# A hybrid attention and mixture-of-experts block: gate and up projections from float32r halves, rows stored modulated, down projection in two banks, last stage in place

## The chip, the cores and the metric

The kernel runs on one core of a Trainium2 chip. The metric is the device time of one execution in microseconds (us), lower is better. A version's time is the median of its runs: the kernel before took 1997.77 us, the median of three runs from 1996.19 to 1998.21.

## The reference

The input is 2048 tokens of width 1024, in float32, and a conditioning vector from which six rows of 1024 come (shift, scale and gate, for each of two halves of the layer). What is computed, cut to what the change touches (`mixed` comes from attention and a short convolution):

```python
mod = silu(c) @ w_ada + b_ada
sh1, sc1, g1, sh2, sc2, g2 = split(mod, 6)
...
x  = x + g1 * (mixed @ w_out)
h2 = rms_norm(x, norm2_g) * (1 + sc2) + sh2
g  = h2 @ w_rg + b_rg                      # 4 groups: the best one is taken
e  = h2 @ w_re + b_re                      # 8 experts in each: the best two of that group
y  = sum over the two experts of gate * ((silu(h2 @ w_gate[e]) * (h2 @ w_up[e])) @ w_down[e])
x  = x + g2 * y
out = rms_norm(x, final_g)
```

There are 32 experts. Each has `w_gate` and `w_up` of 1024x256 and `w_down` of 256x1024: 1 MB each, 96 MB in all, and all of it is read.

## The kernel before, in words

The program is a sequence of stages: projection, attention, mixing (`mix`), ranking of the tokens (`route`), experts (`experts`, L1720) and the last norm (`combine`, L2126). Within a stage the instructions of each engine are written out by hand, engine by engine, and the engines wait for each other by semaphores; an engine takes its instructions strictly in the order written. TensorE is PE, VectorE DVE, ScalarE ACT, GpSimd POOL and SyncE SP.

**Products from halves.** A plain float32 product shows as two records in the trace. In the earlier stages, and in the experts' down projection, both factors are instead split into a high part, which is the value written as float32r, and a low part, which is the rest. Three float32r products (high by high, low by high, high by low) then give the result. ScalarE writes high parts and VectorE or GpSimd subtracts to get low ones.

**`mix`** takes 16 tiles of 128 tokens. For a tile TensorE multiplies the two halves of `mixed` with `w_out` (L1347), VectorE adds both to the residual (`add_attention`, and `add_conv` at L1450 to L1465), and a row `xs`, the residual divided by its root mean square, is stored for the experts. TensorE also turns the rows for the router (`turn_x`) and computes the router's logits (`route`), one and two tiles later. Because `xs` is not yet scaled by `norm2_g * (1 + sc2)` nor shifted by `sh2`, these two are brought to columns at the first tiles: 32 products of one column (`modulation_columns`, L1411) and two sums into `modc`. VectorE then scales the router's weights (`router_scale`, L1493, `wr` to `wrs`), and TensorE multiplies the shift with the weights (`router_shift`, L1418) for a bias that VectorE adds (L1490). The rows of the gates `g1` and `g2` come by row sums over `macc`, two products each (`modulation_rows`, L1405). ScalarE's queue loads the router's weights and biases (L1522 to L1527). The splits of the tiles are at L1533 (ScalarE, high) and L1573 (GpSimd, low).

**`experts`** gives each expert 192 places (`CAP`) for its tokens and works through 16 pairs of experts. A pair's tokens are gathered by GpSimd's indirect transfers: 128 for the even expert, 128 for the odd one, and the remaining 64 of both as one block `xb`. TensorE transposes the blocks in 24 products (L1864 for the even expert with the shared block, 16; L1874 for the odd one, 8) into two banks. VectorE empties the one bank (`copy_in`, L1945) and ScalarE the other (L2080), and both apply scale and shift from `modc` on the way. `gate_up` (L1877 to L1888) then does 32 float32 products of 192 columns, 16 for gate and 16 for up (`KF` is 2 blocks of 128 of the 256 columns, `KD` 8 slices of the 1024):

```python
for w, out, done in ((wg, gate, gate_done), (wu, up, up_done)):
    for f in range(KF):
        for k in range(KD):
            pe.matmul(out[:, f * CAP:(f + 1) * CAP], w[:, b, k, f * P:(f + 1) * P],
                      xT[:, k, cols_of[b]], start=k == 0, stop=k == KD - 1)
```

ScalarE applies silu to gate (L2104), VectorE multiplies with up and splits the result into `ahi` and `alo` (`middle`, L1970 to L1980), and `down` (L1890 to L1894) does 12 products of 512 columns for the first 128 tokens of an expert into two banks (`outa`), and 12 for the other 64 into two more (`outb`). VectorE empties each pair of banks in one instruction of 1024 columns that also multiplies with the token's gate and with `g2row` (`out_first`, `out_rest`, L1983 to L1995), and GpSimd adds the rows to the residual in HBM by indirect transfers (`scatter`). The down weights are split by ScalarE (L2099, 128x2048) and VectorE (L1966). The weights have two buffers each (`wg`, `wu`, `wd`); SP loads gate and up of an expert as soon as the expert two before has done its up products, and the down weights once its split is done (L1774 to L1782).

The order on TensorE is: gate and up of the odd expert, 8 transposes for the next even one, first part of down of the even expert, 8 transposes, the rest of that down, gate and up of the next even expert, 8 transposes for the next odd one, both parts of down of the odd expert (L1923 to L1939). The orders on VectorE (L2052 to L2074) and ScalarE (L2108 to L2123) follow it.

**`combine`** loads the 8 MB of the residual with eight transfers, norms tile by tile into four result buffers `res`, and stores 16 tiles; from the fifth tile on VectorE waits until a result buffer has been stored.

## Time and profile before

| what | value |
|---|---|
| median of three runs | 1997.77 us (1996.19 to 1998.21) |
| the profiled execution: its own time, its span | 1996.46 us, 1994.3 us |
| PE busy | 1801.4 us, 90% |
| DVE busy | 1179.6 us, 59% |
| ACT busy | 855.5 us, 43% |
| POOL busy | 855.5 us, 43% |
| mean DMA traffic over the span | 138 GB/s |
| mixing stage, about | 1063 to 1330 us |
| expert stage, about | 1354 to 1940 us |
| last stage, about | 1949 to 1994 us |

How to read it: one execution was taken by the hardware profiler. Its times count from the start of its span, and its own time is a little longer than the span. "Busy" counts the time in which an engine executes; waits, register and issuing instructions are not in it. In a timeline a row gives start, duration, engine, line, operation, out<-in and shape, and "x32" says that 32 records are put together. Matrix products are given as stationary shape, then moving shape. PEld are the loads of the stationary operand. In a table of stretches the columns are the window and its length, then the busy time of TensorE's products, its weight loads, VectorE, ScalarE and GpSimd, each with the number of instructions, then the granted clock of TensorE as a part of full speed, the mean busy share of the DMA engines, and GB/s.

### The profile page before, as it was taken

To read this page: it belongs to the slowest core of one execution; us is meant where nothing else is said; L and a number is where in the kernel's file an instruction comes from. 1 tells how busy PE (TensorE), PEld (TensorE's weight loads), DVE (VectorE), ACT (ScalarE), POOL (GpSimd) and SP (SyncE) were. 2 spreads that over 40 slices of the span, in tenths; PEclk is the share of its full clock that TensorE was granted. 3 is DMA by queue.
4 is the path that set the end of the run, shared out by engine and by line. 5 is a ranking of instruction groups with operands and counts; after the bars stand their busy time and mean duration, and the time that the engine had idled before them with its cause. 6 is when DMAs were issued, how large, how long until landed. Compare 5 with 4: busy or idle time off the path is not lost. (4 is left out here: it accounts for less than half of the span.)

```text
span 1994.3 us, 26932 instructions
## 1 busy us (share of the span) xinstructions
PE 1801.4 (90%) x8988; PEld 1479.5 (74%) x8988; DVE 1179.6 (59%) x2009; ACT 855.5 (43%) x1520; POOL 855.5 (43%) x887
## 2 busy tenths in 40 slices
PE   2899999997999999999995999965999999999980
PEld 2677878774777777777784788855899898999970
DVE  4597989857666666666644656553444444444444
ACT  3535454326676777677684232311222222222114
POOL 0032314103888888888892111112343443434330
PEclk8899999996999999999997999976999999999995
DMA  7656565530000000000005343414888787878848
GB/s 282 197 143 192 168 181 158 147 102 0 6 9 6 9 8 6 9 9 6 11 9 199 126 158 137 148 43 163 248 248 252 231 248 245 248 236 239 242 94 337
DMA packets 216176, 274.28 MB, mean 138 GB/s; under 512 B 28469, under 2 KB 176144, under 8 KB 215834
## 3 DMA queue, kind: packets, MB, share of 16 engines
q1 hardware_dynamic: 193498, 220.59, 34.1%
q0 software_dynamic: 20224, 52.47, 10.4%
q8 instruction: 43, 0.70, 0.1%
q10 hardware_dynamic: 2368, 0.17, 0.1%
q14 instruction: 43, 0.35, 0.1%
HBM read 229.13 MB, written 60.82 MB: 145 GB/s over the span
## 5 line engine op out<-in xcount | busy, mean ns | idle before, releaser
L1212 POOL TENSOR_TENSOR plo<-KR,phi 128x512 fp32r<-128x512 f32 (+1 forms) x320 | 353.1, 1123 | 44.6 <-ACT KR L1171 44.4
L1020 DVE TENSOR_REDUCE cmax<-tbank 128x1 f32<-128x512 f32 (+2 forms) x320 | 193.3, 605 | 106.8 <-PE tbank L835 101.6
L1170 ACT ACTIVATE phi<-tbank 128x512 fp32r<-128x512 f32 (+1 forms) x320 | 170.9, 534 | 141.8 <-PE tbank L884 137.3
L387 PE MATMUL pbank<-hhi,wslhi 128*128 128x512 f32 x512 | 207.7, 406 | 8.5 <-DVE wsllo L440 8.5
L1946 DVE TENSOR_SCALAR xTe<-ebank,modcol 128x256 f32<-128x256 f32 (+1 forms) x128 | 53.6, 471 | 262.2 <-PE ebank L1864 137.8
L387 PE MATMUL pbank<-hhi,wsllo 128*128 128x512 f32 x512 | 201.5, 394 | 0.0
L387 PE MATMUL pbank<-hlo,wslhi 128*128 128x512 f32 x512 | 201.4, 393 | 0.0
L331 POOL DMA_DIRECT2D wmod<-in_w_ada x64 | 48.5, 758 | 308.2 <-DVE macc L519 297.9
L1886 PE MATMUL ebank<-xTe,wg 128*128 128x192 f32 x1024 | 174.8, 330 | 3.1 <-DVE ahi L1979 1.8
L1886 PEld LDWEIGHTS ebank<-xTe,wg 128*128 128x128 f32 x1024 | 170.9, 193 | 8.0 <-DVE ahi L1979 2.1
L1886 PE MATMUL ebank<-xTe,wu 128*128 128x192 f32 x1024 | 171.6, 326 | 0.0
L1171 ACT ACTIVATE KR<-tbank 128x512 f32<-128x512 f32 (+1 forms) x320 | 169.2, 529 | 0.0
L1886 PEld LDWEIGHTS ebank<-xTe,wu 128*128 128x128 f32 x1024 | 167.3, 190 | 0.0
L2081 ACT ACTIVATE xTe<-ebank,modcol 128x256 f32<-128x256 f32 (+1 forms) x128 | 56.8, 510 | 232.8 <-PE ebank L1864 146.0
L925 PE MATMUL tbank<-phi,VVhi 128*128 128x512 f32 (+1 forms) x320 | 134.7, 421 | 3.8 <-ACT phi L1170 3.7
L835 PE MATMUL tbank<-Khi,Qhi 96*128 96x512 f32 (+2 forms) x320 | 122.1, 384 | 5.4 <-DVE cmax L1020 4.8
L1573 POOL TENSOR_TENSOR mlo<-mixed,mhi 128x1024 fp32r<-128x1024 f32 x16 | 38.4, 2397 | 197.7 <-ACT mhi L1533 197.7
L387 PEld LDWEIGHTS pbank<-hhi,wslhi 128*128 128x128 f32 x512 | 97.4, 190 | 31.9 <-DVE wsllo L440 9.8
L883 PE MATMUL tbank<-Qhi,Klo 96*128 96x512 f32 (+1 forms) x320 | 118.3, 370 | 0.0
L903 PE MATMUL tbank<-plo,VVhi 128*128 128x512 f32 (+1 forms) x322 | 117.9, 366 | 0.3 <-POOL plo L1212 0.2
L884 PE MATMUL tbank<-Qlo,Khi 96*128 96x512 f32 (+1 forms) x320 | 118.1, 369 | 0.0
L926 PE MATMUL tbank<-phi,VVlo 128*128 128x512 f32 (+1 forms) x320 | 117.3, 367 | 0.0
(279 smaller groups left out, 3963.4 us busy)
## 6 DMA issues: line engine op xcount, KB each, us to landing
wg<-in_w_exp_gate SPq DMA_DIRECT2D x32, 1024.0 KB, 5.5
wu<-in_w_exp_up SPq DMA_DIRECT2D x32, 1024.0 KB, 8.9
wd<-in_w_exp_down SPq DMA_DIRECT2D x32, 1024.0 KB, 5.0
wraw<-in_w_in SPq DMA_DIRECT2D x60, 512.0 KB, 4.4
wmod<-in_w_ada POOLq DMA_DIRECT2D x64, 256.0 KB, 3.5
xt<-in_x SPq DMA_DIRECT2D x4, 2048.0 KB, 11.4
wada<-in_w_ada SPq DMA_DIRECT2D x4, 2048.0 KB, 19.7
mixed<-mix_dram SPq DMA_DIRECT2D x16, 512.0 KB, 4.3
```

Source lines behind the costliest of these rows:

```text
L387: ins = pe.matmul(out, w[:, S % 3, k], h[:, n % 2, k], start=k == 0 and j == 0, stop=k == KD - 1 and j == 2)
L835: pe.matmul(plain[:, chunk % 2, 0:w], Qhi[0:QKD, b, i * P:(i + 1) * P], Khi[0:QKD, b, n * 512:n * 512 + w], start=True, stop=True).then_in ...
L883: pe.matmul(out, Klo[0:QKD, b, k], Qhi[0:QKD, b, q], start=False, stop=False)
L884: pe.matmul(out, Khi[0:QKD, b, k], Qlo[0:QKD, b, q], start=False, stop=True).then_inc(scores_done, 1)
L903: ins = pe.matmul(outp[:, g % 2, first_tile(g, kt) * P:512], heads_values(VVhi, kt, b), step_of(plo, m), start=False, stop=last)
L925: pe.matmul(out, heads_values(VVhi, kt, b), step_of(phi, m), start=kt == 0, stop=False)
L926: pe.matmul(out, heads_values(VVlo, kt, b), step_of(phi, m), start=False, stop=False)
L1020: W(ve.tensor_reduce(cmax[:, i % 2, n:n + 1], plain[:, chunk % 2, 0:w], AX.X, ALU.max), plain_read)
L1170: A(act.activation(step_of(phi, m), scores[:, m % 2, j * P:512], ACT.Exp), phi_done)
L1171: A(act.activation(step_of(probs, m), scores[:, m % 2, j * P:512], ACT.Exp), exp_done)
L1212: po.tensor_tensor(step_of(plo, m), step_of(probs, m), step_of(phi, m).bitcast(F32), ALU.subtract).then_inc(plo_done, 1)
L1886: ins = pe.matmul(out[:, f * CAP:(f + 1) * CAP], w[:, b, k, f * P:(f + 1) * P], xT[:, k, cols_of[b]], start=k == 0, stop=k == KD - 1)
```

## The change

It has five parts.

1. **Gate and up from halves.** The gathered rows `xT` are kept as a high and a low part, side by side in the columns, and the weights as `ghi` and `glo`. For every slice one product of `ghi` takes 384 columns (192 of high and 192 of low tokens), and one of `glo` takes the 192 high ones and is added to the first half. A block of gate or up now has a bank of its own, so gate and up take four banks. ScalarE copies the low halves of both out of PSUM (`low_gate`, `low_up`), VectorE adds the high ones (`add_gate`, `add_up`), and silu and `middle` work in SBUF. Gate and up weights have one buffer each, `gu`; ScalarE writes `ghi` and VectorE `glo` in four blocks of 128 columns an expert, each as soon as TensorE has done the same block of the expert before. SP loads gate, up and down weights one after the other as those splits are done.
2. **Rows stored modulated.** `mix` makes rows of scale and shift (`scrow`, `shrow`) at the first tile, by row sums over `macc`, from three more rows that ScalarE's queue loads (two of `b_ada` and `norm2_g`, each spread over the 128 partitions). A stored row is already multiplied and shifted, with one more pass of VectorE a tile. The router takes its weights and biases as they are, and the transposes of the experts are emptied by plain copies and subtractions: ScalarE copies each bank as high part and VectorE subtracts for the low part (`rest_even`, `rest_odd`).
3. **Down projection in two banks.** The two banks `outp` serve both parts of the tokens; the loop over the two blocks of 512 columns is now the outer one, and VectorE empties one block at a time (four instructions of 512 columns in place of two of 1024).
4. **Half of the down split on GpSimd.** VectorE subtracts for the first block of `wd` and GpSimd for the second, between its gathers and scatters.
5. **Last stage in place.** `combine` writes the result over the residual, a partition takes two adjoining rows of 4 KB in one transfer, and eight stores of 1 MB take the place of sixteen.

The core of the diff:

```diff
+                if at == 1:
+                    pe.wait_ge(mod_read, 2)
...
+                    pe.wait_ge(attn_gated, 1)
+                    modulation_rows(1, 4, product[0])
                     pe.wait_ge(mod_read, 1)
-                    modulation_columns()
+                    modulation_rows(1, 2, turn)
...
+                if isinstance(t, int) and t == 0:
+                    modulate_rows()
                 ve.wait_ge(x2_scale, t + 1)
                 ve.wait_ge(st_xs[b], uses(t, b))
-                ve.tensor_scalar(xs[:, b], x2[:, b], xstat[:, b, 2:3], None, ALU.mult).then_inc(xs_ready, 1)
+                ve.scalar_tensor_tensor(xs[:, b], x2[:, b], xstat[:, b, 2:3], scrow[:], ALU.mult, ALU.mult
+                                        ).then_inc(xs_scaled, 1)
+                ve.wait_ge(xs_scaled, t + 1)
+                ve.tensor_tensor(xs[:, b], xs[:, b], shrow[:], ALU.add).then_inc(xs_ready, 1)
...
+            def modulate_rows():
+                ve.wait_ge(ld_srow, 16 * 3)
                 ve.wait_ge(mod_summed, 2)
-                ve.tensor_tensor(modc[:, 16:32], turn[:, 0, 0:16], cols[:, 24:40], ALU.add).then_inc(mod_read, 1)
-                ve.wait_ge(mod_read, 2)
-                ve.scalar_tensor_tensor(modc[:, 24:32], modc[:, 24:32], 1.0, cols[:, R_N2:R_N2 + 8], ALU.add, ALU.mult
+                ve.scalar_tensor_tensor(scrow[:], product[0].rearrange("p a n -> p (a n)"), 1.0, scrow[:], ALU.add, ALU.add
                                         ).then_inc(mod_read, 1)
+                ve.wait_ge(mod_summed, 3)
+                ve.tensor_tensor(shrow[:], shrow[:], turn.rearrange("p a n -> p (a n)"), ALU.add).then_inc(mod_read, 1)
                 ve.wait_ge(mod_read, 3)
-                ve.wait_ge(ld_r, 16 * 4)
-                for k in range(KD):
-                    ve.tensor_scalar(wrs[:, k], wr[:, k], modc[:, 24 + k:25 + k], None, ALU.mult)
-                    ins = ve.tensor_scalar(shift[:, k], cst[:, C_ONE:C_ONE + P], modc[:, 16 + k:17 + k], None, ALU.mult)
-                ins.then_inc(shift_ready, 1)
+                ve.tensor_tensor(scrow[:], scrow[:], xs[:, 1], ALU.mult).then_inc(row_ready, 1)
...
+            act.dma_start(shrow[:], b_ada[0, 3 * D:4 * D].partition_broadcast(P)).then_inc(ld_srow, 16)
+            act.dma_start(scrow[:], b_ada[0, 4 * D:5 * D].partition_broadcast(P)).then_inc(ld_srow, 16)
+            act.dma_start(xs[:, 1], T["norm2_g"][0, :].partition_broadcast(P)).then_inc(ld_srow, 16)
...
-        wg, wu, wd = sb("wg", [P, 2, KD, FE]), sb("wu", [P, 2, KD, FE]), sb("wd", [P, 2, KF, D])
+        gu, wd = sb("gu", [P, 2, KD, FE]), sb("wd", [P, 2, KF, D])
+        ghi, glo = sb("ghi", [P, 2, KD, FE], F32R), sb("glo", [P, 2, KD, FE], F32R)
...
-        turn, gate, up, outa, outb = bank[:, 0:2], bank[:, 2], bank[:, 3], bank[:, 4:6], bank[0:CAPB, 6:8]
+        turn, gate, up, outp = bank[:, 0:2], bank[:, 2:4], bank[:, 4:6], bank[:, 6:8]
...
+            def load_gate(r, i, g):
+                sp.wait_ge(glo_ready, r * (NEXP * 4) + i * (NGRP * 4) + (g * 4 + 2))
+                sp.dma_start(gu[:, 0], wgd[:, bass.ds(i * KD + g * EPG * KD, KD), :]).then_inc(ld_g, 16)
...
+                sp.wait_ge(dlo_pool, r * NEXP + i * NGRP + (g + 1))
...
                     for g in range(NGRP):
-                        b = g % 2
-                        sp.wait_ge(up_done, r * NEXP + i * NGRP + (g + 1))
-                        sp.dma_start(wg[:, b], wgd[:, bass.ds(i * KD + g * EPG * KD, KD), :]).then_inc(ld_gu[b], 16)
-                        sp.dma_start(wu[:, b], wud[:, bass.ds(i * KD + g * EPG * KD, KD), :]).then_inc(ld_gu[b], 16)
-                        sp.wait_ge(dlo_ready, r * NEXP + i * NGRP + (g + 1))
-                        sp.dma_start(wd[:, b], wdd[:, bass.ds(i * KF + g * EPG * KF, KF), :]).then_inc(ld_wd[b], 16)
+                        load_up(r, i + (g + 1) // NGRP, (g + 1) % NGRP)
+                        load_down(r, i + (g + 1) // NGRP, (g + 1) % NGRP)
+                        load_gate(r, i + (g + 2) // NGRP, (g + 2) % NGRP)
...
+            def split_down(q, b, r):
+                hold(po, dhi_ready, r * NEXP + q * 2 + (b + 1), passed_pool)
+                po.tensor_tensor(dlo[:, b, 1], wd[:, b, 1], dhi[:, b, 1].bitcast(F32), ALU.subtract).then_inc(dlo_pool, 1)
...
                 with po.Fori(0, PAIRS - 2) as q:
+                    split_down(q, 1, r)
                     gather_even(q + 2, r)
                     scatter(q, 0, r)
+                    split_down(q + 1, 0, r)
                     gather_odd(q + 2, r)
                     scatter(q, 1, r)
...
+                for m, (out, free) in enumerate(((gate, gate_added), (up, up_added))):
+                    pe.wait_ge(free, r * NEXP + q * 2 + (b + 1))
                     for f in range(KF):
+                        pe.wait_ge(glo_ready, r * (NEXP * 4) + q * 8 + (b * 4 + m * 2 + f + 5))
+                        at, both = slice(f * P, (f + 1) * P), out[:, f, 0:2 * CAP].rearrange("p (h n) -> p h n", h=2)
                         for k in range(KD):
-                            ins = pe.matmul(out[:, f * CAP:(f + 1) * CAP], w[:, b, k, f * P:(f + 1) * P],
-                                            xT[:, k, cols_of[b]], start=k == 0, stop=k == KD - 1)
-                    ins.then_inc(done, 1)
-
-            def down(out, b, lo, hi, done):
+                            pe.matmul(both, ghi[:, m, k, at], xT[:, k, :, cols_of[b]], start=k == 0, stop=False)
+                            ins = pe.matmul(both[:, 0], glo[:, m, k, at], xT[:, k, 0, cols_of[b]],
+                                            start=False, stop=k == KD - 1)
+                        ins.then_inc(unit_done, 1)
...
+            def down(n, b, lo, hi, done):
+                out = outp[0:hi - lo, n]
                 for f in range(KF):
                     for j, (a, w) in enumerate(((ahi, dhi), (alo, dhi), (ahi, dlo))):
-                        for n in range(2):
-                            ins = pe.matmul(out[:, n], a[:, b, f, lo:hi], w[:, b, f, n * 512:(n + 1) * 512],
-                                            start=f == 0 and j == 0, stop=f == KF - 1 and j == 2)
+                        ins = pe.matmul(out, a[:, b, f, lo:hi], w[:, b, f, n * 512:(n + 1) * 512],
+                                        start=f == 0 and j == 0, stop=f == KF - 1 and j == 2)
...
+                for n in range(2):
+                    pe.wait_ge(yb_done, r * (NEXP * 2) + q * 4 + (b * 2 + n + 1))
+                    down(n, b, b * CAPB, b * CAPB + P, down_a)
 
             def down_rest(q, b, r):
-                pe.wait_ge(yb_done, r * NEXP + q * 2 + (b + 1))
-                down(outb, b, 0 if b else P, CAPB if b else CAP, down_b)
+                for n in range(2):
+                    pe.wait_ge(ya_done, r * (NEXP * 2) + q * 4 + (b * 2 + n + 2))
+                    down(n, b, 0 if b else P, CAPB if b else CAP, down_b)
...
+                ve.tensor_tensor(xT[:, 2 * g:2 * g + 2, 1, 0:2 * P], turn[:, g % 2].rearrange("p (k n) -> p k n", k=2),
+                                 xT[:, 2 * g:2 * g + 2, 0, 0:2 * P].bitcast(F32), ALU.subtract).then_inc(turn_dve, 1)
...
+                ve.tensor_tensor(glo[:, m, :, at], gu[:, m, :, at], ghi[:, m, :, at].bitcast(F32), ALU.subtract
...
+                ve.tensor_tensor(sg[:], sg[:], gate[:, :, 0:CAP], ALU.add).then_inc(gate_added, 1)
...
                 with ve.Fori(0, PAIRS - 1) as q:
+                    for f in range(KF):
+                        split_in(q, 1, r, 1, f)
+                    middle(q, 0, r)
                     split_down(q, 0, r)
-                    copy_even(q + 1, r, 0)
+                    split_in(q + 1, 0, r, 0, 0)
+                    add_gate(q, 1, r)
+                    split_in(q + 1, 0, r, 0, 1)
+                    add_up(q, 1, r)
+                    rest_even(q + 1, r, 0)
+                    rest_even(q + 1, r, 1)
+                    out_first(q, 0, r)
+                    rest_even(q + 1, r, 2)
+                    rest_even(q + 1, r, 3)
+                    out_rest(q, 0, r)
+                    for f in range(KF):
+                        split_in(q + 1, 0, r, 1, f)
                     middle(q, 1, r)
-                    copy_even(q + 1, r, 2)
-                    out_first(q, 0, r)
-                    out_rest(q, 0, r)
                     split_down(q, 1, r)
-                    copy_odd(q + 1, r)
-                    middle(q + 1, 0, r)
+                    split_in(q + 1, 1, r, 0, 0)
+                    add_gate(q + 1, 0, r)
+                    split_in(q + 1, 1, r, 0, 1)
+                    add_up(q + 1, 0, r)
+                    rest_odd(q + 1, r, 0)
+                    rest_odd(q + 1, r, 1)
                     out_first(q, 1, r)
                     out_rest(q, 1, r)
...
+                act.activation(ghi[:, m, :, at], gu[:, m, :, at], ACT.Copy).then_inc(ghi_ready, 1)
...
+                act.activation(sg[:], gate[:, :, CAP:2 * CAP], ACT.Copy).then_inc(low_copied, 1)
...
                 with act.Fori(0, PAIRS - 1) as q:
-                    split_down(q, 0, r)
+                    split_in(q + 1, 0, r, 0, 0)
+                    low_gate(q, 1, r)
+                    split_in(q + 1, 0, r, 0, 1)
+                    split_down(q, 1, r)
                     gated(q, 1, r)
-                    copy_even(q + 1, r, 1)
-                    copy_even(q + 1, r, 3)
-                    split_down(q, 1, r)
+                    low_up(q, 1, r)
+                    for g in range(4):
+                        copy_even(q + 1, r, g)
+                    for f in range(KF):
+                        split_in(q + 1, 0, r, 1, f)
...
+            for i in range(NL):
+                sp.wait_ge(normed, 2 * i + 2)
+                sp.dma_start(out_rows[2 * i * P:(2 * i + 2) * P, :].rearrange("(p q) d -> p q d", p=P),
+                             x2[:, 2 * i:2 * i + 2]).then_inc(st_out, 16)
...
-                if t >= NR:
-                    ve.wait_ge(st_out[t % NR], 16 * (t // NR))
-                ve.scalar_tensor_tensor(res[:, t % NR], x2[:, t], stat[:, t, 2:3], fgrow[:], ALU.mult, ALU.mult
+                ve.scalar_tensor_tensor(x2[:, t], x2[:, t], stat[:, t, 2:3], fgrow[:], ALU.mult, ALU.mult
```

## Rows read from the trace of the kernel before

**Rows 1.** Stretches, expert stage: engines' busy us (x instructions), clock, DMA share, GB/s.

```profile
1500.00:1600.00 100.00, 100.00 (x588) 90.82 (x586) 43.88 (x55) 21.14 (x32) 40.16 (x38) 1.00 0.81 244
```

**Rows 2.** Timeline of TensorE and VectorE, one pair of experts: start us, duration.

```profile
1485.18 5.37 PE L1886 MATMUL ebank<-xTe,wg 128*128 128x192 f32 x32
1485.47 1.27 DVE L1986 SCALAR_TENSOR_TENSOR yb<-ebank,gate_b,g2row 64x1024 f32<-64x1024 f32 x1 [1.10 <-PE ebank L1894]
...
1495.59 1.04 PE L1874 MATMUL ebank<-cst,xa 128*128 128x128 f32 x8
...
1501.95 5.36 PE L1886 MATMUL ebank<-xTe,wg 128*128 128x192 f32 x32
...
1519.62 0.65 PE L1886 MATMUL ebank<-xTe,wg 128*128 128x192 f32 x3
```

**Rows 3.** Timeline of TensorE's products (PE) and weight loads (PEld), end of attention.

```profile
1051.17 0.34 PE L882 MATMUL tbank<-Qhi,Khi 101*128 101x384 f32 x1
...
1051.69 0.39 PE L925 MATMUL tbank<-phi,VVhi 128*128 128x512 f32 x1
...
1052.38 0.28 PE L882 MATMUL tbank<-Qhi,Khi 101*128 101x256 f32 x1
...
1052.73 0.34 PE L925 MATMUL tbank<-phi,VVhi 128*128 128x384 f32 x1
...
1053.09 0.39 PE L903 MATMUL tbank<-plo,VVhi 128*128 128x512 f32 x1
...
1053.32 0.22 PE L882 MATMUL tbank<-Qhi,Khi 101*128 101x128 f32 x1
1053.32 0.19 PEld L883 LDWEIGHTS tbank<-Qhi,Klo 96*128 96x128 f32 x1
...
1053.43 0.19 PEld L884 LDWEIGHTS tbank<-Qlo,Khi 96*128 96x128 f32 x1
```

**Rows 4.** Groups of VectorE by form before 1055: busy us, mean ns, idle before.

```profile
L440 DVE TENSOR_TENSOR wsllo<-wraw,wslhi 128x1024 fp32r<-128x1024 f32 x64 | 78.6, 1228 | 24.8 <-ACT wslhi L599 24.6
...
L492 DVE TENSOR_TENSOR z<-pbank,sq 128x512 f32<-128x512 f32 x16 | 10.9, 683 | 0.0
```

**Rows 5.** Groups of ScalarE by form, 1400 to 1900.

```profile
L2099 ACT ACTIVATE dhi<-wd 128x2048 fp32r<-128x2048 f32 x30 | 57.5, 1917 | 0.0
```

**Rows 6.** Groups by form, mixing stage, GpSimd.

```profile
L1573 POOL TENSOR_TENSOR mlo<-mixed,mhi 128x1024 fp32r<-128x1024 f32 x16 | 38.4, 2397 | 197.7 <-ACT mhi L1533 197.7
```

**Rows 7.** DMA issues, 1400 to 1900: KB each, median us to landing.

```profile
wg<-in_w_exp_gate SPq DMA_DIRECT2D x29, 1024.0 KB, 5.5
```

**Rows 8.** Mixing stage: timelines of TensorE and VectorE, stretches, waits.

```profile
1091.17 3.74 PE L1411 MATMUL mbank<-cst,macc_all 128*128 128x1 f32 x32
...
1101.87 1.88 PE L1405 MATMUL mbank<-macc_all,cst 128*128 128x512 f32 x4
...
1109.44 1.95 PE L1418 MATMUL mbank<-wr,shift 128*128 128x36 f32 x16
...
1097.13 0.16 DVE L1462 RECIPROCAL xstat<-xstat 128x1 f32<-128x1 f32 x1
...
1075.00:1080.00 5.00, 5.00 (x18) 3.91 (x18) 3.07 (x3) 2.29 (x3) 0.00 (x0) 0.74 1.02 412
...
DVE term L1454 <- PE mbank L1347: 22.5, 14, 4.8
...
PE mbank L1347 <- DVE rbias L1490: 3.0, 1, 3.0
```

**Rows 9.** Stretches of the last stage.

```profile
1970.00:1975.00 5.00, 0.00 (x0) 0.00 (x0) 1.07 (x1) 0.00 (x0) 0.00 (x0) 0.50 1.02 412
...
1980.00:1985.00 5.00, 0.00 (x0) 0.00 (x0) 4.90 (x10) 4.34 (x11) 0.00 (x0) 0.50 0.90 351
```

**Rows 10.** Timeline of GpSimd and VectorE in the projection stage.

```profile
210.30 1.31 POOL L348 TENSOR_TENSOR hlo<-hf,hhi 128x512 fp32r<-128x512 f32 x1
...
210.58 1.59 DVE L584 TENSOR_TENSOR kvn<-kvn,rq 128x512 f32<-128x512 f32 x1
```

More of the change, by code:

```diff
@@ L2037, in _ @@
                 n = 5
-                for j, (tab, psum, gate) in enumerate(((tab_a, bank[:, 6], gate_a), (tab_b, bank[0:CAPB, 7], gate_b))):
+                for j, (tab, psum, total) in enumerate(((tab_a, bank[:, 6], gate_a), (tab_b, bank[0:CAPB, 7], gate_b))):
                     ve.wait_ge(table_summed, r * 5 + (4 + j))
@@ L2051, in _ @@
                 assert n == TABLE_STEPS
-                copy_even(0, r, 0)
-                copy_even(0, r, 2)
-                copy_odd(0, r)
-                middle(0, 0, r)
+                for m in range(2):
+                    for f in range(KF):
+                        split_in(0, 0, r, m, f)
+                for g in range(4):
+                    rest_even(0, r, g)
+                split_in(0, 1, r, 0, 0)
+                add_gate(0, 0, r)
+                split_in(0, 1, r, 0, 1)
+                add_up(0, 0, r)
@@ L2078, in _ @@
             n_rounds = load_rounds(act)
-            def copy_in(k, at, lo, n):
-                return act.activation(xT[:, k, at], turn[:, 1, lo:lo + n], ACT.Identity,
-                                      scale=modc[:, 24 + k:25 + k], bias=modc[:, 16 + k:17 + k])
             def copy_even(q, r, g):
                 act.wait_ge(turned, r * (PAIRS * 6) + q * 6 + (g + 7))
-                for j in range(2):
-                    ins = copy_in(2 * g + j, slice(0, 2 * P), 2 * j * P, 2 * P)
-                ins.then_inc(turn_act, 1)
@@ L2137, in combine @@
         ld = [sem(f"ld_x2_{b}") for b in range(NL)]
-        st_out = [sem(f"st_out{b}") for b in range(NR)]
+        st_out = sem("st_out")
         squared, scale, normed = sem("squared6"), sem("scale6"), sem("normed")
```

269 lines of the change are left out of this document (155 added, 114 removed).

## The prediction

> **What bounds the kernel now.** I read the expert stage first, since most of the change lies there. In the table of stretches TensorE is busy for all of each 100 us between 1400 and 1900, at a granted clock of 1.00, while VectorE works 44 us, ScalarE 21, GpSimd 40, and the DMA engines 0.81 of the time [rows 1]. So TensorE's own work sets the pace there. The order of its instructions in one pair of experts gives the prices: gate and up of an expert take 1495.59 - 1485.18 = 10.41 us, the eight transposes and the down projection behind them 6.36, and with the even expert's sixteen transposes the pair takes 1519.62 - 1485.18 = 34.44 us [rows 2]. Sixteen pairs are 551 us of the span of 1994.3.
>
> **Gate and up.** A plain float32 product of 192 columns runs as two records: the 16 products of gate are the 32 of its row. The change puts in its place one float32r product of 384 columns (high weights on high and low tokens) and one of 192 (low weights on high tokens). The trace of before has no 192, so I take it from the nearest float32r products, the narrow ones at the end of attention. Three of 384 columns fill 1051.69 - 1051.17 = 0.52 us and two more 0.36 up to 1053.09, 0.176 each; three of 256 take 0.35, 0.117 each [rows 3]. At 128 columns the weight load decides: the load for the next product starts when the present product starts (1053.32), and the one after it 0.11 us later, where 128 columns stream for 0.06 [rows 3]. One load ahead, then, and 0.11 us each. In a train of 384, 192, 384, 192 the load for the low weights hides under the 384 columns, but the load for the next high weights has only the 192 columns to hide under. The 192-column product thus costs 0.11 (as at 128) to 0.117 (as at 256); I take 0.11, since the load, and not the columns, is the longer of the two there, and 0.176 for the wide one. One k-slice: 0.286 us, 32 of them 9.15 us. Gain: 10.41 - 9.15 = 1.26 us an expert, 40.3 us for 32. Bounds: 0.18 + 0.117 gives 9.5 us and a gain of 29; if the load were free, 192 columns at the wide product's rate, 0.088, give 8.45 us and 63.
>
> The loads in these rows start together with a product that fills the same rows of the array, and the down projection with its 24 loads, and eight transposes, fits in 6.36 us [rows 2, 3]. The Trainium skill, "TensorE: Matmul & The Clock Gate", Part 3, "What overlaps and what doesn't", has it otherwise: a weight load overlaps a running product only when its row group differs; by that rule each load here would be paid behind its product and the sum would be that of the last rival below, and the trace does not agree.
>
> Transposes stay. The down projection has the same 24 products, now one output bank at a time; every product already has its own load, so nothing. The two output banks are now shared by both token parts, so TensorE waits for VectorE's evacuation at each turn; below.
>
> **What VectorE, ScalarE and GpSimd must now do beside it.** VectorE gets, per expert: four weight splits of 128x1024 at 1.23 us, half of the down split at 1.23, three remainders of the tokens and four half evacuations at about 0.7 (128x512, one operand in PSUM), two additions and the middle at about 0.55 each for 384 columns [rows 4]: 4.9 + 1.2 + 2.1 + 2.8 + 1.1 + 1.5 = 13.6 us of 15.9. It fits, but only if the order does. From E, the start of gate and up of an expert: VectorE's last half evacuation starts 0.3 later (the hand-over seen at 1485.47 [rows 2]) and ends at 1.0; two up splits end at 3.5, the middle at 5.0, the down half at 6.2, the gate splits with the addition between them at 9.2. TensorE is done at E + 9.15; ScalarE copies the low part (0.5, a quarter of the 1.92 that 2048 elements take [rows 5]), so VectorE's next addition can start at E + 9.9 and has 0.7 us in hand. Then come two remainders and the first evacuation, ready at E + 12.6, and TensorE asks for that bank after transposes and down's first part at E + 9.15 + 0.9 + 2.7 = 12.75: no stall in the odd half, 1 us in hand in the even one. ScalarE: four splits at half of 1.92, the down split 1.92, six smaller ops at 0.5 [rows 5], 9 us of 15.9: hidden. GpSimd takes half of the down split, 2.4 us [rows 6], in a queue that was 40% busy [rows 1].
>
> **Loads.** Gate and up now have one buffer each. The gate load goes out at E + 9.2 and ScalarE needs it 2.6 us into the next expert, at E + 18.5: 9.3 us against a median of 5.5 to landing [rows 7]. DMA use goes from 0.81 to 0.81 x 34.44 / 31.9 = 0.87. I cost it at nothing.
>
> **Mixing stage.** The rows are stored modulated: per tile VectorE gets about 1.75 us more (a second pass over 128x1024 and a dearer first one). It waited for TensorE 22.5 us there, 4.8 at most at one tile [rows 8], and a tile's row is read one tile later: nothing. At the start, the 32 one-column products (3.74 us) become two row sums of 1.88 [rows 8]: equal. The router's shift (1.95) and the wait of 3.0 for the bias go [rows 8]. In their place TensorE waits at tile 1 until VectorE has added the scale row: reciprocal done at 1097.29 [rows 8], one pass over 1024 columns of PSUM, 1.27 as in [rows 2], against TensorE there at 1091.17 + 3.76 = 1094.9: 3.6 us, 3.8 with the hand-over. Sum 3.8 - 1.95 - 3.0 = -1.1. Three broadcast loads of 0.52 MB join queues that already run at 412 GB/s and a share of 1.02 [rows 8]: 3.8 us later weights, on the path; 0 if they slip in before. I take +2.7 for the stage (bounds -1.1 to +4.5).
>
> **Ends.** First transposes of the expert stage: four groups through ScalarE and VectorE in series in place of alternately, +0.6. Last experts: evacuation waits for the last middle, +0.4. Last stage: in place, so VectorE no longer waits for stores; DMA ran at 412 GB/s before 1975 and at 351 from 1980 on [rows 9]; some 20 us at the higher rate save 2.2 (0 to 4; it stays bound by DMA).
>
> **Sum.** -40.3 + 2.7 + 0.6 + 0.4 - 2.2 = -38.8 us. The profiled execution took 1996.46 us (span 1994.3 and 2.2 around it), 1.3 below the median of the three runs, 1997.77. From the median: **1959 us**. This case's own range, with gate and up at 9.0 to 9.4 and the bounds above: 1950 to 1969.
>
> **Rivals.**
> *The loads of weights cost nothing* (0.088 for the narrow product): 63 gained in place of 40, 1936 us. Against it: loads 0.11 apart at 128 columns [rows 3].
> *The port decides* (the other side). When GpSimd ran a two-input pass, VectorE's two-input pass that began 0.28 us behind took 1.59 us where 0.69 is usual; it ended after GpSimd's [rows 4, 10]. The Trainium skill, "SBUF — State Buffer", "Who interferes with whom", states this as a rule: of a VectorE op with two SBUF inputs and a GpSimd op that reads SBUF, the first to start holds the port for its whole length. The trace agrees, 1.59 against 0.69. The point of decision: GpSimd may begin its 2.4 us when ScalarE has written the high down weights, at E + 4.6 + 0.5 + 1.0 + 1.9 + hand-overs = E + 8.5. VectorE's last gate split begins at E + 8.0 if all is as above, so it goes first, and GpSimd runs while VectorE reads PSUM. If VectorE is 0.5 us later, GpSimd goes first, that split ends at 12.1 in place of 9.2, and the addition is 2.2 us late: 2.1 us of stall in the odd half, 1.2 in the even, 3.3 a pair, 53 in all: 2011 us. With the odd half alone 34 us, 1992.
> *The loads are late.* For: one buffer, three loads chained by splits. Were a gate load to take 12.4 us, 3.1 us an expert are lost, 97 in all: 2055. Against: 5.5 [rows 7].
> *A weight load does not overlap*: a slice costs 0.176 + 0.088 + 2 x 0.11 = 0.484 us, an expert 15.5, 5.1 more than before; 163 in all, 2162 us with the other terms. Against it, the loads that start with a running product [rows 3].
>
> **How the numbers follow.** Chances: my sum 0.60; free loads 0.12; port in both halves 0.12, in one 0.07; late loads 0.05; loads not overlapped 0.04. Range for 8 in 10: from the free loads to the port in one half, 1935 to 1992. About 0.2%, 4 us, is what a measurement can tell here. Faster: 0.60 + 0.12 + most of 0.07 = 0.78; same 0.05 (between the two port cases); slower 0.17.
>
> **What would show it.** In the profile after: products of 384 columns 0.17 to 0.18 us apart from the narrow one and 0.11 from the narrow to the next; gate and up 9.15 us; a pair 31.9 us with TensorE without idle at VectorE's evacuations; GpSimd's half split beginning within 0.5 us after the up products end, and no VectorE split longer than 1.3 us; loads landing near 5.5 us; the first products of the mixing stage near 4 us later, a wait of 4 us at tile 1; the last stage at 410 GB/s throughout. I am wrong if a pair is 33 us or more with splits of 2 to 3.6 us (port), if ScalarE waits for gate weights (loads), or if the narrow product starts its successor after 0.09 (free) or 0.2 us (not overlapped).

## The result and the profile after

The changed kernel took 2005.08 us (median of six runs, 2003.94 to 2007.54) against 1998.1 for the kernel before: a ratio of 1.004, with a 95% interval from 1.0029 to 1.0051. It is slower by 7 us where 39 us less were forecast, and outside the stated range.

The profiled execution has a span of 2003.0 us against 1994.3. Laid side by side at seven points of TensorE's timeline, the difference has one place. The third column is a repaired kernel that is explained below (e2); its span is 1943.6.

| stretch | before | after | e2 |
|---|---|---|---|
| start to the first product of mixing | 1074.54 | 1073.01 | 1074.41 |
| to the router's products for tile 0 | 47.91 | 49.46 | 47.13 |
| **to those for tile 15: 15 tiles** | **203.66** | **256.06** | **200.42** |
| to the first gate product of the experts | 56.06 | 53.46 | 54.16 |
| to the last product of the experts | 554.14 | 514.73 | 511.20 |
| to the end | 57.96 | 56.27 | 56.25 |

The expert stage gained 39.4 us, close to the forecast. The fifteen tiles of mixing lost 52.4 and took it all away. First the whole execution and a stretch of the expert stage after (columns as in [rows 1]):

```profile
PE 1790.8 (89%) x8947; PEld 1458.4 (73%) x8948; DVE 1373.2 (69%) x2233; ACT 1000.9 (50%) x1680; POOL 957.2 (48%) x919
1500.00:1600.00 100.00, 100.00 (x634) 90.15 (x634) 82.08 (x110) 55.02 (x70) 64.92 (x51) 1.00 0.87 260
```

TensorE is still busy without a gap there, as in [rows 1], and gets more products done; VectorE went from 44 to 82 us of 100 and keeps up. Two weight slices and one pair of experts, in TensorE's timeline after:

```profile
1625.03 0.25 PE L1912 MATMUL ebank<-xTe,glo 128*128 128x192 f32 x1
1625.03 0.19 PEld L1911 LDWEIGHTS ebank<-xTe,ghi 128*128 128x128 f32 x1
1625.11 0.36 PE L1911 MATMUL ebank<-xTe,ghi 128*128 128x384 f32 x1
1625.14 0.19 PEld L1912 LDWEIGHTS ebank<-xTe,glo 128*128 128x128 f32 x1
1625.31 0.25 PE L1912 MATMUL ebank<-xTe,glo 128*128 128x192 f32 x1
...
1607.94 0.33 PE L1911 MATMUL ebank<-xTe,ghi 128*128 128x384 f32 x1
...
1617.02 0.27 PE L1888 MATMUL ebank<-cst,xa 128*128 128x128 f32 x1
...
1639.74 0.33 PE L1911 MATMUL ebank<-xTe,ghi 128*128 128x384 f32 x1
```

A slice takes 1625.31 - 1625.03 = 0.28 us (0.284 over many), gate and up 1617.02 - 1607.94 = 9.08, a pair 1639.74 - 1607.94 = 31.80.

Now a tile of mixing. This is the part of the kernel before that the front did not show: one tile in the timelines of VectorE, ScalarE and TensorE.

```profile
1233.66 0.75 DVE L1465 TENSOR_SCALAR xs<-x,xstat 128x1024 f32<-128x1024 f32 x1 [0.27 <-ACT xstat L1553]
...
1234.33 0.15 DVE L1436 TENSOR_SCALAR mstat<-mbank 128x2 f32<-128x2 f32 x1
...
1234.72 0.20 ACT L1539 ACTIVATE mstat<-mstat 128x2 f32<-128x2 f32 x1 [1.09 <-DVE mstat L1438]
1234.83 1.01 ACT L1543 ACTIVATE xT<-mbank 128x1024 f32<-128x1024 f32 x1
...
1235.89 1.98 PE L1370 MATMUL mbank<-wrs,xT 128*128 128x36 f32 x16
...
1237.70 0.70 PE L1347 MATMUL mbank<-whi,mhi 128*128 128x512 f32 x2
```

And the same place after:

```profile
1227.23 1.29 DVE L1456 SCALAR_TENSOR_TENSOR xs<-x,xstat,scrow 128x1024 f32<-128x1024 f32 x1 [0.27 <-ACT xstat L1544]
...
1228.55 1.23 DVE L1459 TENSOR_TENSOR xs<-xs,shrow 128x1024 f32<-128x1024 f32 x1
...
1229.69 0.15 DVE L1425 TENSOR_SCALAR mstat<-mbank 128x2 f32<-128x2 f32 x1
...
1230.08 0.20 ACT L1530 ACTIVATE mstat<-mstat 128x2 f32<-128x2 f32 x1 [2.88 <-DVE mstat L1427]
1230.19 1.00 ACT L1534 ACTIVATE xT<-mbank 128x1024 f32<-128x1024 f32 x1
...
1231.25 1.99 PE L1371 MATMUL mbank<-wr,xT 128*128 128x36 f32 x16 [1.68 <-ACT xT L1534]
...
1233.05 1.19 PE L1347 MATMUL mbank<-whi,mhi 128*128 128x512 f32 x2
```

Read it from the bottom. TensorE waited 1.68 us for `xT`, the turned rows that ScalarE copies out of PSUM. ScalarE had nothing else to do: it stood at the root of `mstat`, the scale of the *next* tile's mixers, which is ahead of the copy in its queue. That root waited 2.88 us in place of 1.09 for two tiny instructions of VectorE, and these stand behind the passes that make the stored row, two passes of 1.29 and 1.23 now in place of one of 0.75. None of the three engines needs the row soon; what is late is what stands behind it, two queues further on. In the kernel before the copy ended at 1234.83 + 1.01 = 1235.84 and TensorE began at 1235.89: there was no slack at all. The Trainium skill, "PSUM — Partial Sum Buffer", "Engine vs sequencer instructions", says that the queues of ScalarE, VectorE and GpSimd are strictly first in, first out; these rows agree.

The products behind the wait then take 1.19 us a pair of records where 0.70 is usual. The table of stretches over 1130 to 1300, before and then after, shows why: the granted clock falls from 1.00 to 0.88, so that part of the time runs at its lower level, 1.2 in place of 2.4 GHz.

```profile
1130.00:1300.00 170.00, 170.00 (x911) 143.60 (x911) 100.19 (x132) 52.31 (x84) 28.74 (x12) 1.00 0.42 142
```

```profile
1130.00:1300.00 170.00, 154.87 (x722) 128.34 (x721) 94.28 (x113) 40.58 (x66) 21.37 (x9) 0.88 0.35 117
```

A tile took 14.19 us before and 18.09 after (the mean from the router's products of tile 0 to those of tile 13): 3.90 us lost, of which 1.68 is the wait.

### The profile page after: what moved, and what is told of

The parts are those of the page before. It is cut to its first block and busy times, and to the rows that moved or that the text cites. A ratio compares the mean times of both kernels' runs of the same rounds, so it can differ in the third digit from the quotient of the medians.

```text
span 2003.0 us, 28226 instructions
## 1 busy us (share of the span) xinstructions
PE 1790.8 (89%) x8947; PEld 1458.4 (73%) x8948; DVE 1373.2 (69%) x2233; ACT 1000.9 (50%) x1680; POOL 957.2 (48%) x919
## 5 line engine op out<-in xcount | busy, mean ns | idle before, releaser
L1911 PE MATMUL ebank<-xTe,ghi 128*128 128x384 f32 x1024 | 297.4, 362 | 3.9 <-DVE xTe L1981 2.3
L1912 PE MATMUL ebank<-xTe,glo 128*128 128x192 f32 x1024 | 258.3, 252 | 0.0
L1911 PEld LDWEIGHTS ebank<-xTe,ghi 128*128 128x128 f32 x1024 | 194.8, 190 | 7.4 <-issue 4.5
L1912 PEld LDWEIGHTS ebank<-xTe,glo 128*128 128x128 f32 x1024 | 197.9, 193 | 1.4
L2163 ACT ACTIVATE ghi<-gu 128x1024 fp32r<-128x1024 f32 x128 | 131.8, 1060 | 122.6 <-PE ebank L1912 108.2
L1987 DVE TENSOR_TENSOR glo<-gu,ghi 128x1024 fp32r<-128x1024 f32 x128 | 155.4, 1234 | 7.7 <-ACT ghi L2163 7.4
L599 ACT ACTIVATE wslhi<-wraw 128x1024 fp32r<-128x1024 f32 x64 | 67.6, 1056 | 103.5 <-DMA wraw<-in_w_in 68.0
L1830 POOL TENSOR_TENSOR dlo<-wd,dhi 128x1024 fp32r<-128x1024 f32 x32 | 89.0, 2781 | 62.3 <-ACT dhi L2168 62.3
```

The source lines that it names most:

```text
L1911: pe.matmul(both, ghi[:, m, k, at], xT[:, k, :, cols_of[b]], start=k == 0, stop=False)
L1912: ins = pe.matmul(both[:, 0], glo[:, m, k, at], xT[:, k, 0, cols_of[b]], start=False, stop=k == KD - 1)
L1987: ve.tensor_tensor(glo[:, m, :, at], gu[:, m, :, at], ghi[:, m, :, at].bitcast(F32), ALU.subtract).then_inc(glo_ready, 1)
L2163: act.activation(ghi[:, m, :, at], gu[:, m, :, at], ACT.Copy).then_inc(ghi_ready, 1)
```

## Experiments

**e1 and e2: the two places in the queues.** The theory (Q) was the chain just read. Each of these kernels cuts it at one place and leaves every instruction in. In e1 VectorE's small step goes ahead of the passes, into a gap where VectorE waits for ScalarE's square:

```diff
                 ve.tensor_tensor(x2[:, b], x2[:, b], term[:], ALU.add).then_inc(x2_ready, 1)
+                if not (isinstance(t, int) and t == NT - 1):
+                    mixers_scale(t + 1, 1 - b)
                 ve.wait_ge(x2_squared, t + 1)
...
                 add_conv(t, b)
-                if not last:
-                    mixers_scale(t + 1, 1 - b)
```

> The changed kernel, with VectorE's small step for the next tile's mixer scale (two instructions on one or two columns) put ahead of the two passes that make the stored row; nothing else moves. Theory Q (a queue behind a queue): ScalarE waits for that step, its copy of the turned rows stands behind it, and TensorE's router products wait for the copy, 1.68 us a tile. Then the wait goes, a tile takes 14.2 us as before the change in place of 18.1, and the time is 2005 - 52 = 1953 us (1950 to 1960). Rival V: VectorE's own work per tile, 2.5 us longer for the two passes, sets the pace; an order within VectorE changes nothing, 2005 us. Rival L: the three more row loads or the larger traffic delay the stage; 2005 us too.

It took 1948.06 us: 0.9759 of the kernel before, interval 0.9744 to 0.9774. A tile takes 14.01 us. Q holds, V and L fall.

e2 leaves VectorE alone and puts ScalarE's copy first in the tile:

```diff
+                if not isinstance(t, int) or t >= 1:
+                    copy_x(t - 1, 1 - b)
                 act.wait_ge(x2_ready, t + 1)
                 act.activation(junk[:], x2[:, b], ACT.Square, accum_out=xstat[:, b, 0:1]).then_inc(x2_squared, 1)
...
                     mixers_scale(t + 1, 1 - b)
-                if not isinstance(t, int) or t >= 1:
-                    copy_x(t - 1, 1 - b)
```

> The changed kernel, with ScalarE's copy of the turned rows put ahead of the square of the tile and of the root of the mixer scale; VectorE's order stays as in the change. Theory Q: only the copy's place in ScalarE's queue matters, so TensorE's router products no longer wait, and the time is 1953 us (1950 to 1960). Rival S: the splits of the next tiles, which stay behind the late root on ScalarE, are what TensorE really needs; then the wait turns up at the first product of a tile and the time stays over 1980 us. Rival V: VectorE's work sets the pace, 2005 us.

1946.67 us, 0.9751 (0.9733 to 0.9768). The same stretch in e2:

```profile
1130.00:1300.00 170.00, 169.84 (x920) 145.44 (x918) 120.36 (x144) 55.96 (x85) 28.92 (x12) 1.00 0.43 145
```

VectorE does both passes here and is busy for 120 of 170 us, the clock is back at 1.00. The root still waits 2.88 us for VectorE in each tile; nobody waits for the root any more. So it was the copy's place alone, and S falls too.

**e4: the wait without the change.** The kernel before, with one idle pass in VectorE's queue:

```diff
                 ve.tensor_scalar(xs[:, b], x2[:, b], xstat[:, b, 2:3], None, ALU.mult).then_inc(xs_ready, 1)
+                ve.tensor_tensor(term[:], x2[:, b], g1row[:], ALU.add)
```

> The kernel before, with one more pass of VectorE over 128x1024 (1.23 us, its result is not used) between the stored row and the small step for the mixer scale. Theory Q: the copy that the router's products wait for ended 0.05 us ahead of them in the kernel before, so there is no slack: some 1.1 to 1.2 us of waiting a tile, and by the proportion of the change (52 us for 1.68 us a tile) 34 to 37 us in all, 2032 to 2035 us (2015 to 2045). Rival V: VectorE was busy for 11.5 of 14.2 us a tile and takes the pass in its idle time, 1998 us. Rival L: no load is changed, 1998 us.

2032.18 us, 1.0168 (1.0146 to 1.0190), as Q said. The router's products wait 1.06 us a tile; one of these waits, and the stretch of above:

```profile
1210.93 2.09 PE L1370 MATMUL mbank<-wrs,xT 128*128 128x36 f32 x16 [1.06 <-ACT xT L1544]
```

```profile
1130.00:1300.00 170.00, 159.41 (x782) 132.86 (x782) 95.12 (x121) 43.61 (x70) 23.78 (x10) 0.91 0.37 123
```

A tile takes 16.67 us on the mean, 2.5 more than before: some tiles 15.3, the old time and the wait, most of them 16.9, with the clock at its lower level behind the wait. One pass of 1.23 us made this kernel 34 us slower, on an engine that was idle for two fifths of the stage (in the kernel before it was busy for 100.19 of 170 us there, 8.4 us a tile; the 11.5 of the expectation are in no row).

**e6: the wait filled.** Nine products into a part of a bank that nobody reads, where TensorE waited:

```diff
             def route(t, b):
-                pe.wait_ge(x_copied, t + 1)
-                pe.wait_ge(ld_r, 16 * 4)
                 pe.wait_ge(logit_ready, t)
+                for k in range(9):
+                    pe.matmul(bank[:, 1, P:512], whi[:, 0, 0:P], whi[:, 1, 0:512 - P], start=True, stop=True)
+                pe.wait_ge(x_copied, t + 1)
+                pe.wait_ge(ld_r, 16 * 4)
```

> The changed kernel, with nine products of 384 columns ahead of each tile's router products, into a part of a bank that nobody reads: TensorE works for about 1.6 us where it waited. If a good part of the loss is the clock, which falls to its lower level after the wait (3.9 us a tile lost, of which 1.68 is the wait), the clock stays at 1.00, a tile takes 14.2 + 1.7 = 15.9 us, and the time is 2005 - 28 = 1977 us (1970 to 1985). If the loss is the wait alone, or what follows from it elsewhere, filling it gives nothing: 2005 us or a little more.

1973.64 us, 0.9889 (0.9868 to 0.9909): TensorE does more, and the kernel is 31 us faster than the changed one.

```profile
1130.00:1300.00 170.00, 168.97 (x910) 144.79 (x908) 106.80 (x128) 47.51 (x77) 24.29 (x11) 1.00 0.40 133
```

The clock stays at 1.00 and a tile takes 15.99 us. So of the 3.90 us a tile that the change lost, 18.09 - 15.99 = 2.1 are the clock after the wait, and the remaining 1.8 the place of the wait, which idle products take now.

**e11 and e12: is the move a gain of its own?** e11 makes e2's move in the kernel before; e12 has both moves in the changed kernel.

> A control: the kernel before, with ScalarE's copy of the turned rows put first in the tile, as in the run that did so in the changed kernel. There the copy ended 0.05 us ahead of TensorE, so nothing is waited for that could go; only the weight loads of the router's products, which began late by some 0.2 us a tile (14.20 against 14.01 us a tile), can gain: 13 x 0.2 = 2.5 us, 1995 us against 1998 (same, within what can be told). If the move is a gain of its own and not a repair of what the change did to the queue, some 10 us or more below the kernel before.

1990.16 us, 0.9958 (0.9945 to 0.9972): more than the 3 us expected, though far from 50. In the profiled execution a tile takes 14.01 us in place of 14.19, which is the 2.5 us expected. The expectation overlooked that the kernel before does wait for the copy at tile 14, where it too stands behind other work of ScalarE; the first line is the kernel before, the second e11:

```profile
1319.78 3.46 PE L1370 MATMUL mbank<-wrs,xT 128*128 128x36 f32 x16 [4.47 <-ACT xT L1543]
```

```profile
1321.54 1.98 PE L1370 MATMUL mbank<-wrs,xT 128*128 128x36 f32 x16 [1.11 <-ACT xT L1543]
```

That gives 3.4 us more. From the router's products of tile 0 to the end the profiled execution of e11 is 7.9 us shorter than that of the kernel before. That it took 1996.06 us all the same, the longest of the five, comes from ahead of there: its mixing began 3.4 us later, and the first products of the router came another 4.1 us later. So the move is worth some 8 us by itself. Measured from e11, the rest of the change is worth 0.9746 / 0.9958 = 0.979, 42 us.

> The changed kernel with both moves, VectorE's scale step ahead of the passes and ScalarE's copy first. If either alone removes the whole wait, both together are worth no more than one: 14.0 us a tile, a ratio to the kernel before of 0.975 to 0.976 (1947 us). If each left some wait of the other kind, up to 3 us less.

1947.66 us, 0.9746 (0.9733 to 0.9760): no more than either alone. e2, e1 and e12 cannot be told apart, and each beats both kernels.

The other runs test the terms of the forecast that held; all start from e2.

**e7 and e8: VectorE's slack, and the port.** e7 takes GpSimd's half of the down split away and gives it to VectorE. e8 keeps it and gives VectorE a pass of the same length:

```diff
-                ve.tensor_tensor(dlo[:, b, 0], wd[:, b, 0], dhi[:, b, 0].bitcast(F32), ALU.subtract).then_inc(dlo_ready, 1)
+                ve.tensor_tensor(dlo[:, b, 0], wd[:, b, 0], dhi[:, b, 0].bitcast(F32), ALU.subtract)
+                ve.tensor_tensor(dlo[:, b, 1], wd[:, b, 1], dhi[:, b, 1].bitcast(F32), ALU.subtract).then_inc(dlo_ready, 1)
...
-                po.tensor_tensor(dlo[:, b, 1], wd[:, b, 1], dhi[:, b, 1].bitcast(F32), ALU.subtract).then_inc(dlo_pool, 1)
+                po.sem_inc(dlo_pool, 1)
```

```diff
+                ve.wait_ge(spare_done, r * NEXP + q * 2 + b)
+                ve.tensor_tensor(spare[:], wd[:, b, 0], dhi[:, b, 0].bitcast(F32), ALU.subtract).then_inc(spare_done, 1)
                 ve.tensor_tensor(dlo[:, b, 0], wd[:, b, 0], dhi[:, b, 0].bitcast(F32), ALU.subtract).then_inc(dlo_ready, 1)
```

> The changed kernel with ScalarE's copy first (1947 us), and the whole down split on VectorE: GpSimd does none of it. VectorE gets 1.22 us more an expert. In the trace of the change VectorE idles 1.2 us an expert ahead of its addition to up, behind the splits, so by the queue's order the pass is absorbed there: 1947 us (1944 to 1952). If VectorE's hand-overs were really at their limit (0.7 us in hand, as the prediction had it), 0.5 us a pair of the odd half are lost and more behind them: 1955 to 1965 us.

> The same kernel with GpSimd's half of the down split kept, and one more pass of VectorE of 1.22 us ahead of its own half (result not used). VectorE has as much to do as in the run before, but its last gate split now begins some 0.4 us after GpSimd's split in place of 0.8 us ahead of it. Theory P (of a VectorE pass and a GpSimd pass with two SBUF inputs the later one waits for the other's end): that split ends 2 us later, TensorE waits 1.5 to 3.5 us a pair, and the time is 25 to 60 us above the run before, 1972 to 2007 us. Without such a wait both runs are equal, 1947 us.

e7: 1947.96 us, 0.9766 (0.9749 to 0.9782), equal to e2; a pair still takes 31.80 us. e8: 2007.63 us, 1.0057 (1.0040 to 1.0073), 60 us more for the same work of VectorE. In the timeline after, GpSimd's split starts behind the start of VectorE's last gate split:

```profile
1615.41 1.22 DVE L1987 TENSOR_TENSOR glo<-gu,ghi 128x1024 fp32r<-128x1024 f32 x1
...
1616.22 2.66 POOL L1830 TENSOR_TENSOR dlo<-wd,dhi 128x1024 fp32r<-128x1024 f32 x1 [3.30 <-ACT dhi L2168]
```

In e8 that split starts later, once behind GpSimd's (first two lines, the odd half) and once ahead of it (next two, the even half), and TensorE waits for the evacuation that follows:

```profile
1617.77 2.38 POOL L1831 TENSOR_TENSOR dlo<-wd,dhi 128x1024 fp32r<-128x1024 f32 x1 [3.31 <-ACT dhi L2171]
...
1618.09 3.15 DVE L1988 TENSOR_TENSOR glo<-gu,ghi 128x1024 fp32r<-128x1024 f32 x1
...
1634.88 4.47 DVE L1988 TENSOR_TENSOR glo<-gu,ghi 128x1024 fp32r<-128x1024 f32 x1
...
1635.33 2.92 POOL L1831 TENSOR_TENSOR dlo<-wd,dhi 128x1024 fp32r<-128x1024 f32 x1
...
1641.72 0.45 PE L1921 MATMUL ebank<-dhi,ahi 128*64 128x512 f32 x1 [2.42 <-DVE ya L2036]
```

3.15 and 4.47 us where 1.22 is usual, and a pair of 1646.11 - 1609.48 = 36.63 us (between the starts of gate; the next one takes 35.06). The port case of the prediction is real, and its price was about right: 3.3 us a pair forecast, 60 / 16 = 3.7 measured. The changed kernel met it once, in its first pair (a split of 3.65 us that starts at 1447.04, 0.18 us ahead of GpSimd's), and e2 twice there. In the pairs behind, VectorE's split starts 0.73 us or more ahead of GpSimd's and takes 1.22. That this lead is what spares it is read from the starts in both runs; no run moved the start alone.

**e9: what the narrow product costs.** (In the last slice the wide product also comes behind the narrow one, to close the sum.)

```diff
-                            ins = pe.matmul(both[:, 0], glo[:, m, k, at], xT[:, k, 0, cols_of[b]],
+                            ins = pe.matmul(both[:, 0, 0:P], glo[:, m, k, at], xT[:, k, 0, b * CAP:b * CAP + P],
```

> The changed kernel with ScalarE's copy first, and the low weights applied to 128 tokens of an expert in place of 192: 64 columns less in 32 products an expert; the low weights' share of the other 64 tokens is left out. Theory W (as the prediction priced it): the narrow product costs the 0.11 us between two weight loads and not its columns, a slice stays at 0.286 us, and the time at 1947 us (1944 to 1950). Rival C: columns count, 64 of them are 0.028 us at the rate of the 384 (0.176), 0.9 us an expert and 29 us in all, 1918 us.

1951.11 us, 0.9775 (0.9759 to 0.9791): a third of the narrow product's columns less gains nothing (the interval overlaps that of e2).

```profile
1601.56 0.23 PE L1913 MATMUL ebank<-xTe,glo 128*128 128x128 f32 x1
1601.56 0.19 PEld L1912 LDWEIGHTS ebank<-xTe,ghi 128*128 128x128 f32 x1
...
1601.62 0.39 PE L1912 MATMUL ebank<-xTe,ghi 128*128 128x384 f32 x1
1601.67 0.19 PEld L1913 LDWEIGHTS ebank<-xTe,glo 128*128 128x128 f32 x1
...
1601.85 0.22 PE L1913 MATMUL ebank<-xTe,glo 128*128 128x128 f32 x1
```

The wide product now comes 0.06 us behind the narrow one in place of 0.08, but the next narrow one 0.23 behind the wide in place of 0.20: a slice keeps its 0.29. The columns of the narrow product do not count, then. What stays the same with 128 and 192 columns is the 0.11 us from one weight load to the next (1601.56 and 1601.67 here, 1625.03 and 1625.14 in the changed kernel), as the prediction priced it.

**e10: the last stage.** e2 with `combine` of the kernel before.

> The changed kernel with ScalarE's copy first, and the last stage of the kernel before. From the last product of TensorE to the end it took 58.2 us before and 56.3 with the change, so 1947 + 2 = 1949 us; if the difference came from the experts' last additions and not from the last stage, 1947.

1949.44 us, 0.9771 (0.9754 to 0.9787). The difference of 2.8 us to e2 lies within the intervals; from TensorE's last product to the end its profiled execution takes 1946.84 - 1889.76 = 57.1 us against 56.25 in e2. With the new last stage this stretch takes 55.5 to 56.4 us in the profiled executions of the eight other kernels here that have it, so the profiles give 0.7 to 1.6 us to the last stage.

## Why the prediction was wrong

**The step that failed** is in the mixing stage: "It waited for TensorE 22.5 us there, 4.8 at most at one tile [rows 8], and a tile's row is read one tile later: nothing." Both halves of the sentence are true, and neither decides. VectorE's idle time did hide its own work; but 1.8 us of lateness on VectorE were passed on to whoever waited for the next instruction in its queue. The prediction asked who reads the row. It did not ask what stands behind the row on VectorE, who waits for that, and what stands behind that waiter in turn. The sum took +2.7 us for the stage; the fifteen tiles alone measured +52.4, 3.5 each. The view that had it was the table of waits of the kernel before, which lists the router's weight loads as waiting for this very copy:

```profile
PEld mbank L1370 <- ACT xT L1543: 10.8, 15, 4.7
```

Fifteen waits, one a tile, small (0.4 us each besides the longest, (10.8 - 4.7) / 14), and on the engine that set the pace of the stage. A resource that is waited for in every tile, however briefly, has no slack.

The second part of the miss is that a wait on TensorE was nowhere priced with the clock. It costs over twice its length here: 3.90 us for 1.68, 2.5 for 1.06 in e4.

**The terms that held.** Gate and up: 9.08 us for 9.15 forecast, a pair 31.80 for 31.9, and 39.4 us gained from the first gate product to the last product, where the terms gave 40.3 less 0.4. In e2 it was 42.9, 2.8 of the difference being the first slices, which ran there at 0.28 us at the higher clock and took 0.53 in the changed kernel. That is not the repair: e10 and e12, which have it too, show the slow first slices and gain 39.6 and 39.4. The price of the narrow product, 0.11, held (e9), though not by the sign that the prediction gave for it: the wide product starts 0.08 us behind the narrow one, where 0.11 was forecast and 0.09 was to mean that loads are free. The 0.11 shows in the starts of the loads, not of the products; the sum of a slice and e9 decide. VectorE's order held: GpSimd's split started 1616.22 - 1607.94 = 8.28 us after the start of gate, forecast 8.5, no split collided behind the first pair's, and from 1500 to 1900 TensorE waited for nothing. The addition had even more room than the 0.7 us forecast: VectorE idled 1.2 to 1.3 us ahead of it, and e7 used that up at no loss. The loads land later than assumed, gate in 8.1 us median against 5.5 in [rows 7], so of the 9.3 us in hand 1.2 are left. Between 1500 and 1900 ScalarE did wait for gate weights twice (5.9 us at 1515.69, 8.5 at 1772.86), which was to be a sign of late loads, but the pairs there took 31.80 us like the others. (The price of that rival is a slip: 3.1 us an expert are 99 us for 32, not 97, and give 2058 us, not 2055.)

**The small terms.** The start of mixing was forecast at +2.7 (-1.1 to +4.5): in e2, where nothing else is in the way, it is 47.13 - 47.91 = -0.8, and the first product is not late. That is one execution against one, and the same stretch took 51.97 us in e11, which has the code of the kernel before but for the place of one copy, so less than some 4 us cannot be told here. Nor did the parts hold one by one, so it is luck that the sum stayed within the bounds. Of the two waits that were feared, that for the scale row is 0.2 us at tile 1 of the changed kernel, and the three row loads are followed in e2 by 1.10 + 0.45 us of waiting for the split weights of tile 0. The two row sums, forecast equal to the 3.74 us of the columns, take 6.77:

```profile
1095.10 6.77 PE L1407 MATMUL mbank<-macc_all,cst 128*128 128x512 f32 x8 [0.59 <-DVE x L1434]
```

The start of the experts was forecast at +0.6 and is -1.9 (e2) to -2.6: the first gather of the shared block landed sooner. Before, six weight loads of 1 MB had been issued ahead of it, with the change three; the first line of each pair is GpSimd's issue, the second TensorE's first product. Before:

```profile
1368.33 1.03 POOL L1789 DMA_INDIRECT xb<-xs_dram,ib  x1 [0.30 <-issue]
...
1376.68 0.47 PE L1863 MATMUL ebank<-cst,xa 128*128 128x128 f32 x1 [9.30 <-DMA xb<-xs_dram,ib]
```

After:

```profile
1420.89 1.03 POOL L1803 DMA_INDIRECT xb<-xs_dram,ib  x1 [0.30 <-issue]
...
1425.91 0.47 PE L1888 MATMUL ebank<-cst,xa 128*128 128x128 f32 x1 [5.78 <-DMA xb<-xs_dram,ib]
```

8.35 us from issue to use became 5.02. That fewer loads ahead of it are the cause was not tried. The last stage: the end came 1.7 us sooner, forecast 2.2 for the stage; e10 gives the stage 0.7 to 1.6.

**The sum.** Had the router's copy not stood behind the root, the forecast would have been 1959 us for a kernel that takes 1947: 12 us too careful. In the two profiled executions the tiles (200.42 in place of 203.66, small waits gone too that the kernel before had already) are 3.2 of it, the start of mixing 3.5, that of the experts 2.5 and the experts themselves 3.0, less 0.5 at the end; the start of mixing and the experts differ by as much between executions. **The rivals** named the right kind of event, a wait that takes the place of a gain, in the wrong stage: of the experts only the first pair saw a split collide, no load cost time, and no weight load was left uncovered.

## What to carry to other kernels

When a step on a non-critical engine grows, do not stop at "it was idle" or "its result is needed later": follow its queue. What is the next instruction behind it, who waits for that, and what stands behind the waiter in its own queue, until the chain ends at the engine that sets the pace; there, read the end of the last link against the start of its user in the trace, since a difference of 0.05 us is no slack. A small instruction on which another engine's queue hangs belongs ahead of long passes, and a copy that the pacing engine needs belongs ahead of anything that can wait.

## What the hardware showed that was not expected

A wait of 1.06 us (e4) or 1.68 us (the change) on TensorE once a tile, between products that were otherwise without a gap, cost another 1.4 and 2.1 to 2.2 us a tile by the lower clock that followed (0.91 and 0.88 granted over the stretch); filling it with idle products (e6) gave 31 us back.

In e8 VectorE's pass that started 0.45 us ahead of GpSimd's took 4.47 us all the same, and ended at 1639.35, 1.1 us after GpSimd's end at 1638.25; the one that started 0.32 us behind it also ended 1.1 us after GpSimd's end. The Trainium skill, "SBUF — State Buffer", "Who interferes with whom", has it that the order of issue decides who blocks. The rows agree where GpSimd started first; where VectorE's record starts first by 0.18 or 0.45 us they do not show that VectorE kept the port (it took 3.65 and 4.47 us), while with a lead of 0.73 us or more it took its usual 1.22. The record's start alone does not tell which of the two got the port.
